# Gate rows spread over partitions by way of DRAM instead of by TensorE, VectorE and ScalarE

## The reference

```python
def post_norm_update(x, y, mod, j, g, b):
    gate = mod[:, 3 * j + 2][:, None, :]
    return layer_norm(ALPHA * x + gate * y, g, b)

def half_ffn_sublayer(x, mod, j, wi, wo, g, b):
    y = 0.5 * swiglu(modulate(x, mod, j), wi, wo)
    return post_norm_update(x, y, mod, j, g, b)
```

## Time and profile before

| | us |
|---|---|
| median of three runs | 1713.12 |
| lowest and highest | 1709.82, 1723.11 |
| the profiled execution | 1720.18 |
| its span | 1718.5 |
| PE busy | 1623.8 (94%) |
| DVE busy | 1219.6 (71%) |
| ACT busy | 811.5 (47%) |
| POOL busy | 130.0 (8%) |
| DMA, mean | 201 GB/s |
| granted PE clock, mean | 0.97 of full speed |

### The profile page before, as it was taken

One profiled execution on the slowest core, in us unless ns is written; L12 is line 12 of the kernel. 1 busy time (PEld: TensorE's weight loads), 2 busy tenths in 40 slices (PEclk: granted clock), 3 DMA queues, 4 the chain that ended last, 5 costly groups with the idle time before them and its releaser, 6 DMA issues.

```text
span 1718.5 us, 23912 instructions
## 1 busy us (share of the span) xinstructions
PE 1623.8 (94%) x7663; PEld 1319.0 (77%) x7663; DVE 1219.6 (71%) x1899; ACT 811.5 (47%) x1256; POOL 130.0 (8%) x191
## 2 busy tenths in 40 slices
PE   6989989999889999999999798999999999989997
PEld 5877778777778878888787467887888877668876
DVE  6877888887877775777667757776577755375555
ACT  5465535556444453544534555444444442254442
POOL 1100001100001110011000011110011100000000
PEclk9999989999989999999999999999999998999999
DMA  9763449743568876588645016887488863256551
GB/s 318 260 207 122 156 142 325 251 141 122 180 214 278 278 263 207 177 278 278 224 159 211 25 50 228 277 278 246 145 263 276 280 223 108 80 165 190 178 184 59
DMA packets 199330, 345.72 MB, mean 201 GB/s; under 512 B 10852, under 2 KB 127900, under 8 KB 198732
## 3 DMA queue, kind: packets, MB, share of 16 engines
q1 hardware_dynamic: 174668, 252.90, 44.7%
q0 software_dynamic: 24576, 91.73, 16.8%
HBM read 343.54 MB, written 1.05 MB: 201 GB/s over the span
## 4 chain that ended last, share of the span: by engine, by line
PE 86%; DVE 8%; issue 3%; ACT 2%; DMA 0%; SPq 0%; DVEq 0%; ACTq 0%
PE acc L536 25%; PE acc L538 24%; PE acc L537 24%; DVE w_lo L1447 2%; PE score L660 2%; PE turn L871 1%; PE acc L772 1%; PE acc L1029 1%; PE score L752 1%; PE score L648 1%; PE score L960 1%; DVE att_work L2007 1%; PE score L859 1%; PE turn L761 1%; PE score L816 0%
## 5 line engine op out<-in xcount | busy, mean ns | idle before, releaser
L1447 DVE TENSOR_TENSOR w_lo<-raw,w_hi 128x1024 fp32r<-128x1024 f32 (+1 forms) x490 | 585.4, 1199 | 293.3 <-ACT w_hi L1072 287.2
L1072 ACT ACTIVATE w_hi<-raw 128x1024 fp32r<-128x1024 f32 (+1 forms) x490 | 508.0, 1042 | 561.4 <-PE acc L538 561.1
L536 PE MATMUL acc<-w_hi,xT_hi 128*128 128x512 f32 (+1 forms) x1456 | 589.2, 405 | 23.1 <-DVE xT_lo L1494 8.5
L538 PE MATMUL acc<-w_hi,xT_lo 128*128 128x512 f32 (+1 forms) x1456 | 574.4, 394 | 0.0
L537 PE MATMUL acc<-w_lo,xT_hi 128*128 128x512 f32 (+1 forms) x1456 | 573.8, 394 | 0.0
L536 PEld LDWEIGHTS acc<-w_hi,xT_hi 128*128 128x128 f32 x1456 | 279.7, 192 | 84.4 <-issue 26.5
L538 PEld LDWEIGHTS acc<-w_hi,xT_lo 128*128 128x128 f32 x1456 | 278.7, 191 | 59.0
L537 PEld LDWEIGHTS acc<-w_lo,xT_hi 128*128 128x128 f32 x1456 | 280.0, 192 | 55.4 <-issue 1.2
L453 POOL DMA_DIRECT2D mod_raw<-in_mod_w x144 | 104.0, 723 | 983.7 <-DVE mod_run L1567 797.4
L536 PE MATMUL acc<-w_hi,hT_hi 128*128 128x512 f32 x440 | 174.7, 397 | 0.8 <-DVE hT_lo L1915 0.8
L538 PE MATMUL acc<-w_hi,hT_lo 128*128 128x512 f32 x440 | 174.0, 395 | 0.0
(11 more groups left out here) (260 smaller groups left out, 1305.8 us busy)
## 6 DMA issues: line engine op xcount, KB each, us to landing
raw<-in_ffn_wi SPq DMA_DIRECT2D x220, 512.0 KB, 5.0
mod_raw<-in_mod_w POOLq DMA_DIRECT2D x144, 512.0 KB, 4.4
raw<-in_ffn_wo SPq DMA_DIRECT2D x110, 512.0 KB, 4.5
raw<-in_w_in SPq DMA_DIRECT2D x72, 512.0 KB, 5.3
raw<-in_w_out SPq DMA_DIRECT2D x16, 512.0 KB, 4.5
raw<-in_attn_wqkv SPq DMA_DIRECT2D x16, 512.0 KB, 4.7
wide<-in_b_merge POOLq DMA_DIRECT2D x4, 1024.0 KB, 9.0
raw<-in_w_branch_a SPq DMA_DIRECT2D x8, 512.0 KB, 4.1
```

The lines of the kernel that those rows point to most:

```text
L536: nc.tensor.matmul(dst, xh, wh, start=start, stop=False)
L538: return nc.tensor.matmul(dst, xl, wh, start=False, stop=stop)
L1072: nc.scalar.activation(w_hi[:, i % SPLIT_SLOTS, 0:n], raw[:, s, i % 2 * PIECE:i % 2 * PIECE + n], ACT.Copy).then_inc(hi_ready, 1)
L1447: nc.vector.tensor_tensor(w_lo[:, i % SPLIT_SLOTS, 0:n], raw[:, i // 2 % RAW_SLOTS, i % 2 * PIECE:i % 2 * PIECE + n], w_hi[:, i % SPLIT_SL ...
```

## The change

The gate's values go from their 128 partitions to a row in DRAM (`gate_vectors`, one row per use) by one DMA, and from there to all partitions by a second one, both issued by POOL. POOL waits for `mods_ready` (the vector is there), then issues the store, waits for it to land (`gate_out`), and issues the broadcast. `post_norm` waits for `gate_in`. The factor 0.5 or 1.0 moves into the scaling, which becomes a three-operand operation. `mods_ready` is raised by a memset of one column after each store of modulation vectors. PE's, DVE's and ACT's `gate_rows` and the tile `gate_diag` go, with all their calls. POOL gets one more wait: it waits for the first block's `x_ready` before the context block's gate, ahead of the weights `mods_of(1, 0)`.

```diff
+        gate_vectors = nc.dram_tensor("gate_vectors", (N_GATES, D), F32).ap()
...
-        gate_diag = sb("gate_diag", [P, KD, P])
...
+            def gate_load(mod, j, stored):
+
+
+                n = c.now("gate")
+                v = (3 * j + 2) * KD
+                pool.wait_ge(mods_ready, stored)
+                pool.dma_start(gate_vectors[n].rearrange("(k p) -> p k", p=P), mod[:, v:v + KD], allow_slow_non_contiguous=True).then_inc(gate_out, 16)
+                pool.wait_ge(gate_out, 16 * c.next("gate"))
+                pool.dma_start(gate_row[:], gate_vectors[n].partition_broadcast(P)).then_inc(gate_in, 16)
...
             norm_rows(a["ln_g_2"][0, 0], a["ln_b_2"][0, 0])
+            gate_load(mod_lat[:, 0, :], 0, LAYERS)
             mods_of(0, 2)
+            pool.wait_ge(x_ready, c.next("x", 2))
+            gate_load(mod_ctx, 0, LAYERS)
             mods_of(1, 0)
             pool.wait_ge(ctx_ready, 2)
             pool.dma_start(qkv_bias[:], a["attn_bqkv_2"][0].partition_broadcast(P)).then_inc(att_in, 16)
             pool.dma_start(band[:], a["band"].rearrange("(t p) n -> p t n", p=P)).then_inc(band_in, 16)
             norm_rows(a["ln_g_2"][0, 1], a["ln_b_2"][0, 1])
+            gate_load(mod_lat[:, 0, :], 1, LAYERS)
             for u in range(AH // 2):
                 pool.wait_ge(out_scaled, u + 1)
                 nc.gpsimd.tensor_copy(xT_hi[:, u, :], att_out[:, u % 2, :]).then_inc(out_hi, 1)
                 pool.wait_ge(out_hi, u + 1)
                 nc.gpsimd.tensor_tensor(xT_lo[:, u, :], att_out[:, u % 2, :], xT_hi[:, u, :].bitcast(F32), ALU.subtract).then_inc(out_split, 1)
-            c.next("x", 2)
             pool.wait_ge(x_ready, c.next("x", 2))
             norm_rows(a["ln_g_2"][0, 2], a["ln_b_2"][0, 2])
+            gate_load(mod_lat[:, 0, :], 2, LAYERS + 1)
             pool.dma_start(dft_ch, a["dft_ch"].rearrange("(k p) n -> p k n", p=P)).then_inc(dft_in, 16)
             pool.dma_start(dft_tok, a["dft_tok"].rearrange("(k p) n -> p k n", p=P)).then_inc(dft_in, 16)
             mods_of(1, 1)
             pool.wait_ge(x_ready, c.next("x", 2))
             norm_rows(a["ln_g_2"][1, 0], a["ln_b_2"][1, 0])
+            gate_load(mod_lat[:, 1, :], 0, LAYERS + 2)
             mods_of(1, 2)
             pool.wait_ge(x_ready, c.next("x", 2))
             norm_rows(a["ln_g_2"][1, 1], a["ln_b_2"][1, 1])
+            gate_load(mod_lat[:, 1, :], 1, LAYERS + 3)
             pool.wait_ge(x_ready, c.next("x", 2))
             norm_rows(a["ln_g_2"][1, 2], a["ln_b_2"][1, 2])
+            gate_load(mod_lat[:, 1, :], 2, LAYERS + 4)
...
-            def gate_rows():
-
-                pe.wait_ge(diag_ready, c.next("diag"))
-                for n in range(2):
-                    b = SCORE[n]
-                    nc.tensor.matmul(take(b)[:], ones[:], gate_diag[:, 4 * n:4 * n + 4, :], start=True, stop=True).then_inc(full[b], 1)
...
-                gate_rows()
...
-            def gate_rows():
-                for n in range(2):
-                    nc.scalar.activation(gate_row[:, n * 512:n * 512 + 512], filled(SCORE[n])[:], ACT.Copy).then_inc(moved[SCORE[n]], 1)
...
+            def mods_stored():
+                nc.vector.memset(free[:, 0:1], 0.0).then_inc(mods_ready, 1)
+
             def kept_store(l, j):
                 at = slice(3 * j * KD, 3 * j * KD + 4 * MOD_KEPT)
                 nc.vector.tensor_tensor(mod_lat[:, l, at], filled("score1")[:, 0:4 * MOD_KEPT], modb[:, l, at], ALU.add).then_inc(moved["score1"], 1)
+                mods_stored()
...
                 mod_store(*ctx_chunk(4))
+                mods_stored()
...
-            def gate_rows(mod, j, factor):
-
-                dve.wait_ge(moved["score1"], c.now("score1") + 1)
-                for k in range(KD):
-                    v = (3 * j + 2) * KD + k
-                    m = nc.vector.tensor_scalar(gate_diag[:, k, :], ident[:], mod[:, v:v + 1], factor, ALU.mult, ALU.mult)
-                m.then_inc(diag_ready, 1)
-                for b in SCORE:
-                    c.next(b)
-                c.value["gate"] = c.now("score1") + 1
-
-            def post_norm(x, ready, last_pieces, rows=32, first_half=None, **splits):
-
-                dve.wait_ge(moved["score1"], c.now("gate"))
+            def post_norm(x, ready, factor, last_pieces, rows=32, first_half=None, **splits):
+
+                dve.wait_ge(gate_in, 16 * c.next("gate"))
                 def gate(t, n):
                     at, b = slice(n * 512, n * 512 + 512), ACC[2 * n + t]
-                    nc.vector.tensor_tensor(gated[:, t, at], bank[b][:], gate_row[:, at], ALU.mult).then_inc(moved[b], 1)
+                    nc.vector.scalar_tensor_tensor(out=gated[:, t, at], in0=bank[b][:], scalar=factor, in1=gate_row[:, at],
+                                                   op0=ALU.mult, op1=ALU.mult).then_inc(moved[b], 1)
...
-                post_norm(x, ready, KF, rows, **end)
+                post_norm(x, ready, 0.5, KF, rows, **end)
...
-                gate_rows(mod_lat[:, 0, :], 1, 1.0)
...
-                gate_rows(mod_lat[:, 1, :], 1, 1.0)
...
-                post_norm(x, x_ready, 4, first_half=lambda: products(4), **by_tile)
+                post_norm(x, x_ready, 1.0, 4, first_half=lambda: products(4), **by_tile)
```

More of the change, by code:

```diff
@@ L73 @@
 MOD_RING = 2
+N_GATES = 7
 MOD_KEPT = 3 * D // 512
@@ L308, in program @@
         silu_done = sem("silu_done")
-        diag_ready = sem("diag_ready")
+        mods_ready = sem("mods_ready")
+        gate_out = sem("gate_out")
+        gate_in = sem("gate_in")
         k_twice_ready = sem("k_twice_ready")
@@ L1895, in ffn @@
             def ffn(x, ready, mod, j, mods=None, rows=32, then=False, end={}, early=0):
-                gate_rows(mod, j, 0.5)
                 def chunk(half, features=(), n=4, into=None):
```

## The result

The changed kernel takes 1728.12 us (median of 20 runs, 1721.72 to 1733.24) and the kernel before, on the same chips, 1723.15 (20 runs, 1709.82 to 1729.87). The ratio is 1.0036, interval 1.0018 to 1.0053 (the two medians alone would give 1.0029): slower by 0.4%, where a gain of 0.6% (1703 of 1713) was forecast. The median of the three runs of before that were shown lay 10 us under its median of 20, so 10 of the 25 us by which the forecast missed are level, and 15 are the change. The profiled spans point the same way: 1718.5 before, 1725.5 after. The 20 times of before lie in two groups, 6 from 1709.8 to 1716.8 and 14 from 1720.5 to 1729.9, and of the three shown two belong to the first, where none of the changed kernel's 20 lies.

A forecast was written before the change was run, and what follows sets the result against it. TensorE was taken as the bound, 86% of the span; 8.6 (feed-forward) + 2.6 (Fourier) - 1.0 (late loads) = 10.2 us gained, from the 1713.1 median to 1703 us (profiled execution 1720.2 to 1710); range 1694 to 1720.

The forecast's parts named there:

- S: On POOL's queue, time from the gate store's issue until POOL sees it landed; forecast 7 us, 8 behind the norm rows.
- the late blocks: Four blocks whose modulation loads queue behind POOL's wait; only the third was forecast late, by 0.8, taken as 1 us.
- limits: Longest store time before the first partial product is late: 16.8 first, 9.7 context, 7.2 third, 10.9 us fourth block.
- the slow store: Rival, chance 0.13: the store holds back modulation loads in four blocks; at 17.6 us 14.6 us slower, 1728, up to 1737.
- break-even: Store time of 13.0 us, at which late modulation loads cost 11.2 us and eat the whole forecast gain.
- Five feed-forward blocks: PE's gate passes stand in the chain of each; removing them gains 5 x 1.72 = 8.6 us.
- The cover rival: PE then waits for splits or partial products, so only the Fourier block's 2.6 us stay: 1710.5; chance 0.13.
- DVE, ACT, the three-operand scaling and the memsets: In feed-forward blocks, removed blocks and copies, the scaling's new form and six added memsets all counted as nothing.
- Attention: In the attention block PE's 1.72 us of gate passes lie beside DVE work, so nothing is gained.
- Fourier: In the Fourier block DVE's 1.57 us of diagonal blocks and 1.0 of PE's 1.72 us are gained, together 2.6 us.
- The clock rival: Fourier block: a shorter PE wait leaves the clock at 2.4 GHz, 3.3 us more gained, 1700; chance 0.14.
- Within 1%: Whole kernel: no change that could be told, neither under 1696 nor over 1730 us; chance 0.84.

The follow-up runs named there:

- e1: Changed kernel with POOL issuing each block's modulation loads ahead of the gate's store, wait and broadcast (DFT loads first too); 1704.97 us, ratio 0.9901.
- e9: Changed kernel with each gate store as 512 pieces of 8 bytes instead of 1024 of 4, values in another order; one run, 1716.96 us.
- e10: Changed kernel storing only the first half of each gate, 512 pieces of 4 bytes, spread to both halves by two broadcasts; one run, 1729.93 us.
- e11: Changed kernel with the gate stores issued by ACT at each block's start; POOL's wait and broadcast stay; one run, 1726.58 us.
- e2: As e1, but only the first gate is stored and broadcast, and all seven scalings use that row; 1705.31 us, ratio 0.9909.
- e3: Changed kernel with each gate store as 128 pieces of 32 bytes instead of 1024 of 4, values in another order; 1706.75 us, ratio 0.9911.
- e4: Kernel before, gate rows made as ever, plus only POOL's seven gate stores and the waits for them, no broadcast; 1732.25 us, ratio 1.0041.
- e5: Changed kernel with each gate store issued ahead of POOL's norm row loads, its wait and broadcast still behind them; 1724.98 us, ratio 1.0014.
- e7: e1 with DVE's eight diagonal-block operations put back in the Fourier block alone, their result unread; one run, 1711.24 us.

## Why the prediction was wrong

**The step that failed is the price of S and of what follows it.** The prediction took S as 7 us (8 in the third block), and the landing of the loads as 6 (7 behind the DFT loads), and put the late blocks at 1.0 us. Its limits compare as follows (us; how late the product is counts from the start of each block; e1 has the same work with the loads on time):

| block | S: limit, measured | broadcast to product: used, measured | product late | PE waits | longer than e1 |
|---|---|---|---|---|---|
| first | 16.8, 16.4 | 7.3, 9.5 | 1.7 | 0.4 | 1.6 |
| context | 9.7, 10.3 | 7.3, 9.8 | 3.4 | 1.3 | 1.5 |
| third | 7.2, 12.9 | 9.8, 13.3 | 9.3 | 8.6 | 10.8 |
| fourth | 10.9, 12.9 | 7.3, 9.9 | 4.5 | 5.3 | 7.1 |
| sum | | | 18.9 | 15.6 | 21.0 |

A term of 1.0 us measured 21.0. S, 10.3 to 16.4, was in the upper half of the bounds, not near lam_const's 5.5 us: that was a load, and of 16-byte pieces, and e9 and e10 show that the price of a store jumps between 8 bytes and 4. "Nearest in piece size" was the wrong way to choose when the size differed by four. The second column was missed for another reason: the prediction charged the broadcast 0.55 us for its issue and nothing for its own 512 KB in front of the loads, and did not see that the store stops the weight loads, which then all run at once when the modulation loads go out (363 GB/s from 712 to 714 us). With the forecast S and the measured second column, only the third block would be late by more than 0.1, by 0.8 + 3.5 = 4.3 us. With the measured S and the forecast column, the third, fourth and context block would be late by 5.7, 1.8 and 0.9, 8.4 together. Neither alone gives 18.9. What PE waited is less than the lateness by some slack. In the third and fourth block the loss is some 2 us more than the wait, which goes with the low clock behind it (0.50 from 1080 to 1084 us); the sum had no term for that, and the rival only at its upper end.

The prediction's estimate from the Trainium skill's figures, 12.8 us, is near the 12.9 of the third and fourth block, but by luck: it has a packet for each of 1024 pieces, and neither half the pieces (e10) nor 32 packets or 1040 (e11) change the time.

**The rival that came true is the slow store**, at 0.13. The mechanism, its place and the worst block were as described, the size was not: break-even was put at S = 13.0 in the context, third and fourth block, and there it was 10.3, 12.9 and 12.9. With the rival's own 7.3 and 9.8 us behind the store that is 8.4 us of lateness, less than the 11.2 of the gain. It is the second column that made the kernel slower.

**Five feed-forward blocks, 8.6 us: right in the sum.** With the loads on time (e1) they are 8.7 us shorter together (1.9, 0.1, 1.4, 3.2, 2.0), in e2 and e3 8.2 and 8.3. The cover rival (0.13) is dead: PE is without work for 4.0, 1.0, 1.4, 1.0 and 7.4 us of the five blocks before and for 4.0, 1.0, 1.4, 1.0 and 7.2 in e1, so no wait came in the place of the passes. That the single blocks differ from 1.72 is the clock: it is 0.99 before and 0.98 in e1 in the context block, which gains 0.1, and 0.98 and 0.99 in the fourth, which gains 3.2. So near a sum is partly luck.

**DVE, ACT, the three-operand scaling and the memsets: nothing, right.** The scaling is 684 ns against 682 before, a memset 59 ns. Also right: the broadcast is never waited for at the block's end.

**Attention, 0: right, as far as the clock lets it be seen.** The +0.2 us of the changed kernel is a sum of two. Up to the end of PE's wait of some 4 us, near 950 us, the block is 1.6 us shorter than before, with a clock of 1.00 in its first 8 us where it was 0.82; behind the wait it is 1.8 longer, with 0.74 in 10 us where it was 0.83. In e1, which is 1.3 longer, it is the first part (1.6 longer, clock 0.72). In e2 and e3, both some 1.9 longer, it is the second (1.9 longer, clock 0.53), and in e4, which keeps all gate passes, it is both. Where the clock at the start is nearest to that of before (e5, 0.83) the wait ends 54.2 us into the block, as before: the removed passes change nothing there. Why the clock stays low for longer in one execution than in another was not settled.

**Fourier, 2.6 us: right in its terms, too small in the sum.** DVE's 1.57 went; of PE's 1.72, 0.75 was gained (1.0 forecast), since the last bank's copy is next, as said. The clock rival (0.14) was true: 8.48 to 5.43 us, 3.1 of the 3.3 us that it named. "The wait only shrinks by half" was taken as a reason against it; e7 shows that this half was just what counted. The whole block is 5.1 us shorter in the changed kernel and 6.8 in e1, with the same 5.43 us for the 12 products.

**The chances.** "Within 1%" had 0.84 and is what happened. The time lay outside 1694 to 1720 because the loss and the level of the three runs came together, and the range had no room for both: three runs say little of the level when they lie 13 us apart. The 1% (17 us) under which the prediction saw no change that could be told was too coarse: 20 runs of each kernel told 0.4%.

## What to carry to other kernels

Before a wait is put on a queue, list what is queued behind it and who needs that first; issue those ahead of the wait (e1: one move of lines, from 0.4% slower to 1% faster). Price a store by the size of its pieces, not by its bytes, and measure it by itself where no row comes within a factor of two: a store in pieces of 4 bytes took more than three times as long here as the same data in 32-byte pieces, and all but stopped other transfers meanwhile. A wait of PE can cost more than its length: 3.4 us brought the low clock here, and 1.8 us did not (e7, e1).

## What the hardware showed

- A 4 KB store in 4-byte pieces lands 10.0 us after its issue (10.5 when ACT issues it), a 2 KB one 10.6; behind norm rows S was up to 16.4. The profile counts 32 packets for POOL's store and 1040 for ACT's. In 8-byte pieces it is 4.5, in 32-byte ones 2.9. Why the step lies between 4 and 8 bytes stays open.
- While such a store is under way the core moves 19 to 35 GB/s, and 512 KB weight loads issued then take 13.7 us instead of 4.4 (e3) or 4.7 (before).
- PE's clock after a wait of 1.8 us stays at 2.4 GHz in the Fourier block; after 3.4 us (before, e4, e7) it drops to 1.2 GHz and the next 12 products take 6.9 to 8.5 us instead of 5.4.
